# Two mixture-of-experts loops: down products on four 32-column tiles and up weights in runs of eight rows per partition

## The chip, the cores and the metric

The kernel runs on one core of a Trainium2 chip, in float32. The metric is the time of one execution on the device in microseconds. TensorE is called PE in the profile's rows (its weight loads PEld), VectorE DVE, ScalarE ACT, GpSimd POOL and SyncE SP.

## The reference, cut to what matters

The program is two transformer blocks on 1024 tokens of width 1024. Each block ends with a mixture of experts: a router picks two of 32 experts for each token, the pairs are sorted by expert and padded to whole blocks, and each block of tokens goes through one expert.

```python
def moe_ffn(u, rg_w, rg_b, re_w, re_b, w1, w3, w2):
    ...
    xb = u[row_tok].reshape(n_blocks, MOE_BLOCK, u.shape[1])

    def expert_block(args):
        xblk, e = args
        return (jax.nn.silu(xblk @ w1[e]) * (xblk @ w3[e])) @ w2[e]

    yb = lax.map(expert_block, (xb, block_expert)).reshape(n_rows, u.shape[1])
    y = yb[dest] * sw[:, None].astype(u.dtype)
    return jax.ops.segment_sum(y, stok, num_segments=n_tok)
```

In the first block `w1` and `w3` are 32 x 1024 x 512 and `w2` is 32 x 512 x 1024; in the second block (`hier_moe`, the same formula) the hidden width is 256. The input of the experts is the block's normed activation: in the first block `modulate(rms_norm(x, g), shift, scale)`, in the second `rms_norm` with a gain. The first block's result is also multiplied by a gate vector of 1024 elements.

## The kernel before

The kernel cuts the sorted pairs into blocks of 96 tokens (`BT`), and the number of blocks is found at run time: with these inputs 36 in the first loop and 32 in the second. `phase_experts` (L1559) is one function for both, called with a hidden width of 512 (four groups of 128, `HT = 4`) or 256 (`HT = 2`). Its loops run over pairs of blocks, with two slots `s` in every buffer. The engines work by semaphores, each in its own program order:

- SP loads the weights of the next block but one. L1586 moves `w1` and `w3` into `wu[:, s, j]` once TensorE has freed them (`wufree`), then L1588 moves `w2` into `wd` (`wdfree`). All are laid out by `experts_to_tiles` (L158): partition p gets the rows k x 128 + p, k = 0 to 7. Each descriptor is one row, 2 KB or 1 KB of `w1` and `w3`, 4 KB of `w2`.
- POOL fetches the 96 tokens of the next block: it copies the block's column of token numbers (L1605) and issues an indirect transfer of 96 rows of 4 KB from `keep_normed` in DRAM into `xg` (L1607). It starts when TensorE has transposed the tokens that were in the other slot (`xt`).
- TensorE does the up products of block i (L1634: for each of `w1` and `w3`, each group of 128 hidden columns and each k, two products on column tiles of 64, moving operand `uT[:, s, k, :]` of 96 tokens), then `turn` (L1620), eight transposes of the next block's tokens, then waits for `hT` (`gated`), for the weights and for a free result tile (`yout`), and does the down products (L1646): 2 halves of 512 columns x `HT` products with `hT` (128 x 96 tokens) as the stationary operand. They use 96 of the array's 128 columns. In the profile each float32 product is two records (a transpose is one), so the first loop has 256 records at L1634, 8 at L1620 and 16 at L1646 a block.
- ACT does silu of the first up result (L1668), scales the transposed tokens into `uT` with a factor and an addend for each partition and k (L1657), in the second loop copies the results to `yo` (L1677), and issues the transfer of 96 rows to `keep_rows` (L1679).
- DVE multiplies silu by the second up result into `hT` (L1695); in the first loop it also multiplies the result by the gate into `yo` (L1701).

The stationary operand of transpose k is `xg[:, slot, k*P:(k+1)*P]`, 128 neighbouring elements of each token. Input channel k x 128 + p so lands on partition p of group k, where the weights' row k x 128 + p is.

Ahead of each expert loop come the route phase (`phase_mix_route`) and, before it, the merge phase (`phase_merge`), which has a list of copies on POOL's queue: `copy_aside` (L119) issues them one by one; the first `needed` are issued at once, and POOL waits for each later one to land before it issues the next. In the profile `mixed_T` and `b2z_Z` are the memory of `wd` in the first and the second loop; `in_w` as a source in the second loop stands for `w1_2`, `w3_2` and `w2_2`.

## Time and profile before

| | us |
|---|---|
| time, median of 3 runs | 4847.99 |
| lowest and highest | 4840.06, 4849.69 |
| the profiled execution, its own time | 4835.41 |
| its span in the profile | 4833.6 |
| TensorE busy (share of the span) | 4203.8 (87%) |
| DVE busy | 1292.3 (27%) |
| ACT busy | 1027.0 (21%) |
| POOL busy | 467.5 (10%) |
| first expert loop, from and to | 1804.7, 2502.5 |
| second expert loop, from and to | 4429.8, 4786.5 |

The span is 1.8 us shorter than the profiled execution's own time, and that execution is 12.6 us below the median. The page cuts the span into 40 slices of 121 us: the first loop lies in the 16th to the 21st, the second in the last four. Busy shares are means over stages with different limits, so what bounds a loop has to be read from its own rows: from the timeline of one engine, where a bracket behind a row gives the idle time before it and what ended that. A timeline row joins instructions of one kind that follow each other, and its length ends with the last one's end, which may lie behind the start of the next row. A row of the table of stretches has the stretch, its length, the busy time (and number of instructions) of PE, PEld, DVE, ACT and POOL, TensorE's granted clock as a share of 2.4 GHz, the busy share of the DMA engines and their GB/s.

### The profile page before, as it was taken

To read this page: it belongs to the slowest core of one execution; us is meant where nothing else is said; L and a number is where in the kernel's file an instruction comes from. 1 tells how busy PE (TensorE), PEld (TensorE's weight loads), DVE (VectorE), ACT (ScalarE), POOL (GpSimd) and SP (SyncE) were. 2 spreads that over 40 slices of the span, in tenths; PEclk is the share of its full clock that TensorE was granted. 3 is DMA by queue.
4 is the path that set the end of the run, shared out by engine and by line. 5 is a ranking of instruction groups with operands and counts; after the bars stand their busy time and mean duration, and the time that the engine had idled before them with its cause. 6 is when DMAs were issued, how large, how long until landed. Compare 5 with 4: busy or idle time off the path is not lost. (4 is left out here: it accounts for less than half of the span.)

```text
span 4833.6 us, 90330 instructions
## 1 busy us (share of the span) xinstructions
PE 4203.8 (87%) x38805; PEld 2639.6 (55%) x38805; DVE 1292.3 (27%) x2325; ACT 1027.0 (21%) x2418; POOL 467.5 (10%) x672
## 2 busy tenths in 40 slices
PE   7897588987899979999979886998999979997885
PEld 2343244876344447777755443448888834445663
DVE  2425112123000130110123554225665520112002
ACT  2200100013000012211223332014444300012333
POOL 1010000000000000000010000005445400000001
PEclk9999799997899989999989998999999989998998
DMA  5361211000411139999973001100000031115998
GB/s 201 140 184 59 102 39 61 31 14 0 133 46 30 51 104 378 367 369 368 369 280 86 9 5 61 35 17 3 4 4 4 4 116 46 30 60 163 353 351 300
DMA packets 361717, 601.08 MB, mean 124 GB/s; under 512 B 35224, under 2 KB 211895, under 8 KB 358040
## 3 DMA queue, kind: packets, MB, share of 16 engines
q1 hardware_dynamic: 324511, 454.52, 27.9%
q0 software_dynamic: 28592, 115.88, 7.3%
q10 hardware_dynamic: 8394, 27.46, 1.5%
q8 instruction: 174, 2.85, 0.2%
q14 instruction: 46, 0.38, 0.0%
HBM read 522.57 MB, written 75.24 MB: 124 GB/s over the span
## 5 line engine op out<-in xcount | busy, mean ns | idle before, releaser
L1634 PE MATMUL experts_bank<-experts_uT,ex_wu 128*64 128x96 f32 x13312 | 568.5, 247 | 69.7 <-DMA ex_wu<-in_w 41.1
L1634 PEld LDWEIGHTS experts_bank<-experts_uT,ex_wu 128*64 128x64 f32 x13312 | 556.9, 138 | 125.6 <-issue 125.6
L1646 PE MATMUL experts_bank<-mixed_T,experts_hT 128*96 128x512 f32 x576 | 255.9, 597 | 0.0
L1811 PE MATMUL taps_bank<-rwkvh_hT,taps_w 128*128 128x512 f32 x480 | 211.6, 599 | 31.7 <-DMA taps_w<-in_w_in 25.6
L1275 DVE TENSOR_TENSOR merge_pr<-merge_bank,merge_sg 128x512 f32<-128x512 f32 x64 | 44.3, 692 | 709.4 <-ACT merge_sg L1262 435.8
L1695 DVE TENSOR_TENSOR experts_hT<-experts_si,experts_bank 128x384 f32<-128x384 f32 (+1 forms) x68 | 31.3, 460 | 756.6 <-PE experts_bank L1634 756.6
L1248 PE MATMUL merge_bank<-b2m_hT,merge_w 128*128 128x512 f32 x512 | 222.3, 592 | 0.0
L1248 PE MATMUL merge_bank<-mix_h2T,merge_w 128*128 128x512 f32 x512 | 222.3, 592 | 0.0
L1811 PE MATMUL hin_bank<-mix_hT,hin_w 128*128 128x512 f32 x384 | 170.2, 602 | 14.6 <-DMA hin_w<-in_w_in 8.9
L1811 PEld LDWEIGHTS taps_bank<-rwkvh_hT,taps_w 128*128 128x128 f32 x480 | 90.6, 191 | 152.7 <-issue 146.3
L2081 POOL TENSOR_TENSOR rc_lev<-rc_arb,rwkv_level 128x256 f32<-128x256 f32 x192 | 153.8, 834 | 157.3 <-DVE rc_arb L2434 157.2
L1646 PEld LDWEIGHTS experts_bank<-mixed_T,experts_hT 128*96 128x96 f32 x576 | 90.9, 163 | 136.5 <-issue 134.1
L1248 PEld LDWEIGHTS merge_bank<-mix_h2T,merge_w 128*128 128x128 f32 x512 | 97.3, 190 | 122.5 <-issue 122.5
L1248 PEld LDWEIGHTS merge_bank<-b2m_hT,merge_w 128*128 128x128 f32 x512 | 97.3, 190 | 122.5 <-issue 122.5
L1262 ACT ACTIVATE merge_sg<-merge_bank,all_cols 128x512 f32<-128x512 f32 x64 | 44.0, 687 | 546.3 <-PE merge_bank L1248 546.2
L2450 DVE TENSOR_TENSOR rc_xy<-rc_xy,rc_bank 128x256 f32<-128x256 f32 x288 | 120.8, 421 | 122.4 <-PE rc_bank L2095 116.7
L1657 ACT ACTIVATE experts_uT<-experts_bank,all_mod 128x96 f32<-128x96 f32 x296 | 99.5, 442 | 203.9 <-PE experts_bank L1620 203.9
L1248 PE MATMUL merge_bank<-mix_hT,merge_w 128*128 128x512 f32 x256 | 114.9, 602 | 30.2 <-DMA merge_w<-in_hy_w_o 26.0
L327 PE MATMUL vproj_bank<-vproj_w,mix_hT 128*128 128x256 f32 x512 | 114.0, 386 | 23.0 <-DMA vproj_w<-in_w_in 21.6
L1811 PEld LDWEIGHTS hin_bank<-mix_hT,hin_w 128*128 128x128 f32 x384 | 72.9, 192 | 111.4 <-issue 111.4
L2832 PE MATMUL mh_sc<-mla_KTs,mh_QT 128*128 128x512 f32 x256 | 120.7, 594 | 5.1 <-ACT mla_KTs L2877 5.1
L507 PE MATMUL qk_bank<-mix_hT,qk_w 128*128 128x512 f32 x256 | 113.8, 603 | 9.3 <-DMA qk_w<-in_w_in 8.1
(499 smaller groups left out, 6539.5 us busy)
## 6 DMA issues: line engine op xcount, KB each, us to landing
ex_wu<-in_expert_w SPq DMA_DIRECT2D x72, 2048.0 KB, 14.4
mixed_T<-in_expert_w SPq DMA_DIRECT2D x36, 2048.0 KB, 15.4
ex_wu<-in_w SPq DMA_DIRECT2D x64, 1024.0 KB
b2z_Z<-in_w SPq DMA_DIRECT2D x32, 1024.0 KB, 15.9
keep_rows<-experts_yo ACTq DMA_DIRECT2D x68, 384.0 KB, 6.0
keep_rows<-mix_hyT POOLq DMA_DIRECT2D x27, 768.0 KB, 4.7
mix_hT<-in_ada_w POOLq DMA_DIRECT2D x8, 2048.0 KB, 8.6
merge_w<-in_w_in SPq DMA_DIRECT2D x32, 512.0 KB, 5.1
```

Source lines behind the costliest of these rows:

```text
L327: last = pe.matmul(bk[t][:, 0:width], xT[:, k, tok0 + t * P:tok0 + (t + 1) * P], wt[:, s, k, :], start=(k == 0), stop=(k == kt - 1))
L507: last = pe.matmul(bk[2 * s + h][:, :], wt[:, s, k, :], xT[:, k, h * HALF:(h + 1) * HALF], start=(k == 0), stop=(k == KT - 1))
L1248: last = pe.matmul(bk[4 * h + j][:, :], w[:, s, k0 + k, :], x[:, k, hh], start=(k == 0), stop=(k == n - 1))
L1262: act.activation(sg[:, h, j, :], bk[4 * h + j][:, :], ACT.Sigmoid, bias=K.cols[:, bass.ds(i * 2 + (s + gate_col + 8 * j), 1)]).then_inc(si ...
L1275: dve.tensor_tensor(pr[:, h, j, :], bk[4 * h + 2 + j][:, :], sg[:, h, j, :], ALU.mult).then_inc(prod, 1)
L1634: last = pe.matmul(bk[2 + j][c:c + 64, h * BT:(h + 1) * BT], wu[:, s, j, k, h * P + c:h * P + c + 64], uT[:, s, k, :], start=(k == 0), sto ...
L1646: last = pe.matmul(bk[5 + j][0:BT, :], hT[:, k * BT:(k + 1) * BT], wd[:, s, k, j * HALF:(j + 1) * HALF], start=(k == 0), stop=(k == HT - 1))
L1657: last = act.activation(uT[:, slot, k, :], bk[k // 4][:, k % 4 * BT:(k % 4 + 1) * BT], ACT.Identity, scale=scale(k), bias=shift(k) if shif ...
L1811: last = pe.matmul(bk[s * 2 + h][:, :], wt[:, s, k, :], xT[:, k, h * HALF:(h + 1) * HALF], start=(k == 0), stop=(k == KT - 1))
L2081: gp.tensor_tensor(lev[d][:, l, :, :], arb[d][:, :, 0, :], W.level[:, d, l:l + 1, :].to_broadcast([P, J, CH]), ALU.mult).then_inc(pos[d], 1)
L2450: dve.tensor_tensor(xy[d][:, x, :, :], xy[d][:, x, :, :], b2(bk[d][bank]), ALU.add).then_inc(dvs[d], 1)
L2832: last = pe.matmul(sc[g % 2][:, half(x)], QT[:, h % 2, u * P:(u + 1) * P], KTs[:, h // 2 % 2 * 2 + h % 2, half(x)], start=True, stop=True)
```

## The change

The down products go on four tiles of 32 columns instead of one product of 96 columns. The stationary operand is 32 tokens of `hT`. Tiles 0, 1 and 2 take one group of 32 tokens each and columns 0 to 767 of the result (`WIDE`), first 512 and then 256 columns wide. Tile 3 takes columns 768 to 1023 for all three groups of tokens, 256 wide, one group after the other. The results of a block lie in banks 4 + 2s and 5 + 2s instead of always in 5 and 6. `yo` becomes 128 partitions x 768: its partitions 96 to 127 hold the three groups' last quarter. The rows are saved by two transfers, 96 x 768 and 32 x 3 x 256. The gate is laid out in the same way once before DVE's loop (`gt`, four copies).

`w1` and `w3` are laid out by `experts_to_runs`: partition p gets the rows 8p to 8p + 7, which are neighbours in DRAM, so a matrix is 128 descriptors of 16 KB in the first loop and 8 KB in the second. To match, transpose k takes every eighth element of a token, from element k on. Scale and addend for L1657 have to be by the same order: `modrun` is made from `K.mod` by a copy to DRAM (`keep_mod`) and back at the end of the first merge's list of copies, and `ffnrun` by a load at the end of the second's. `w2` stays as it was. The diff, cut to its core:

```diff
             gp.dma_start(dst, src).then_inc(asided, 16)
...
+def experts_to_runs(ap):
+    return ap.rearrange("l e (p k) n -> p (l e) k n", p=P)
...
+OUT = ((0, HALF), (HALF, WIDE))
...
-        yo = m.sb("yo", [BT, 2, D])
+        yo = m.sb("yo", [P, 2, WIDE])
+        gt = m.sb("gt", [P, WIDE]) if gate is not None else None
...
-                    last = pe.transpose(bk[k // 4][:, k % 4 * BT:(k % 4 + 1) * BT], xg[:, slot, k * P:(k + 1) * P], K.ident[0:BT, 0:BT])
+                    last = pe.transpose(bk[k // 4][:, k % 4 * BT:(k % 4 + 1) * BT], xg[:, slot, :].rearrange("q (p k) -> q k p", k=KT)[:, k, :], K.ident[0:BT, 0:BT])
...
+            def quarter(s, j, c, tokens, k, c0, n, at):
+                return pe.matmul(bk[4 + 2 * s + j][32 * c:32 * c + 32, at:at + n], hT[:, k * BT + 32 * tokens:k * BT + 32 * tokens + 32],
+                                 wd[:, s, k, c0:c0 + n], start=(k == 0), stop=(k == HT - 1))
...
                     for j in range(2):
+                        width = HALF if j == 0 else 256
+                        rest = [(t, k) for t in ((0, 1) if j == 0 else (2,)) for k in range(HT)]
                         for k in range(HT):
-                            last = pe.matmul(bk[5 + j][0:BT, :], hT[:, k * BT:(k + 1) * BT], wd[:, s, k, j * HALF:(j + 1) * HALF], start=(k == 0), stop=(k == HT - 1))
+                            for c in range(3):
+                                last = quarter(s, j, c, c, k, j * HALF, width, 0)
+                            for t, q in rest[k * len(rest) // HT:(k + 1) * len(rest) // HT]:
+                                last = quarter(s, j, 3, t, q, WIDE, 256, t % 2 * 256)
                         last.then_inc(ymm, 1)
...
-                        act.activation(yo[:, s, j * HALF:(j + 1) * HALF], bk[5 + j][0:BT, :], ACT.Copy).then_inc(yout, 1)
+                        act.activation(yo[:, s, OUT[j][0]:OUT[j][1]], bk[4 + 2 * s + j][:, 0:OUT[j][1] - OUT[j][0]], ACT.Copy).then_inc(yout, 1)
...
+                    act.dma_start(rows[:, 0:WIDE], yo[0:BT, s, :]).then_inc(saved[s], 16)
+                    act.dma_start(rows[:, WIDE:D].rearrange("(g p) n -> p g n", p=32), yo[BT:P, s, :].rearrange("p (g n) -> p g n", g=3)).then_inc(saved[s], 16)
...
+            if gate is not None:
+                dve.tensor_copy(gt[0:BT, :], gate[0:BT, 0:WIDE]).then_inc(gates, 1)
+                for g in range(3):
+                    dve.tensor_copy(gt[BT:P, g * 256:(g + 1) * 256], gate[BT:P, WIDE:D]).then_inc(gates, 1)
+                dve.wait_ge(gates, 4)
...
-                            dve.tensor_tensor(yo[:, s, j * HALF:(j + 1) * HALF], bk[5 + j][0:BT, :], gate[0:BT, j * HALF:(j + 1) * HALF], ALU.mult).then_inc(yout, 1)
+                            dve.tensor_tensor(yo[:, s, a:z], bk[4 + 2 * s + j][:, 0:z - a], gt[:, a:z], ALU.mult).then_inc(yout, 1)
...
-    ws = tuple(experts_to_tiles(I[w]) for w in (w1, w3, w2))
+    ws = (experts_to_runs(I[w1]), experts_to_runs(I[w3]), experts_to_tiles(I[w2]))
...
+                    + ((S.mod.rearrange("a (k p) -> p a k", p=P), K.mod[:, 2, :, :]), (K.modrun[:, :, :], S.mod.rearrange("a (p k) -> p a k", p=P))), 5)
...
+                        + ((K.ffnrun[:, :], I["norm_ffn_g_2"].rearrange("l (p k) -> p (l k)", p=P)),), 4, crossed=True)
```

What stands in a row on TensorE in the second half of the second loop's body, one block, before (up products, a wait, eight transposes, a wait, four down products):

```order
L1634 MATMUL experts_bank<-experts_uT,ex_wu 64x96 x64
L1637 REGISTER_ALU
L1620 MATMUL experts_bank<-all_ident,ex_xg 128x96 x8
L1641 REGISTER_ALU
L1646 MATMUL experts_bank<-b2z_Z,experts_hT 96x512 x4
L1648 REGISTER_ALU
```

The same place of the changed kernel:

```order
L1649 MATMUL experts_bank<-experts_uT,ex_wu 64x96 x64
L1652 REGISTER_ALU
L1630 MATMUL experts_bank<-all_ident,ex_xg 128x96 x8
L1656 REGISTER_ALU
L1635 MATMUL experts_bank<-b2z_Z,experts_hT 32x512 x3
L1635 MATMUL experts_bank<-b2z_Z,experts_hT 32x256 x2
L1635 MATMUL experts_bank<-b2z_Z,experts_hT 32x512 x3
L1635 MATMUL experts_bank<-b2z_Z,experts_hT 32x256 x10
L1668 REGISTER_ALU
```

The up products and transposes stand as they did. The 4 down products of 96 columns have become 18 of 32: 3 of 512 columns for tiles 0 to 2, then 2 of 256 for tile 3, twice over, and then, joined with these in the last row, 3 of 256 for tiles 0 to 2 and 1 for tile 3, twice over.

ACT in the same half of the body, before (silu, the scaling of the next tokens, the two result copies, the transfer of the rows):

```order
L1668 ACTIVATE experts_si<-experts_bank 128x192
L76 REGISTER_ALU
L1657 ACTIVATE experts_uT<-experts_bank,all_cols 128x96 x8
L1677 ACTIVATE experts_yo<-experts_bank 96x512
L76 REGISTER_ALU
L1677 ACTIVATE experts_yo<-experts_bank 96x512
L1678 REGISTER_ALU
L1679 ISA
L1679 DMA keep_rows<-experts_yo 96x1024
```

And of the changed kernel:

```order
L1688 ACTIVATE experts_si<-experts_bank 128x192
L76 REGISTER_ALU
L1677 ACTIVATE experts_uT<-experts_bank,all_ffnrun 128x96 x8
L1697 ACTIVATE experts_yo<-experts_bank 128x512
L76 REGISTER_ALU
L1697 ACTIVATE experts_yo<-experts_bank 128x256
L1698 REGISTER_ALU
L1700 ISA
L1700 DMA keep_rows<-experts_yo 96x768
L1701 ISA
L1701 DMA keep_rows<-experts_yo 32x3x256
```

The second copy is half as wide as the first, both are 128 partitions high, and behind them stand two transfers instead of one.

## Rows read from the trace of the kernel before

**Rows 1.** The page's line of what the DMA engines moved, in 40 slices.

```profile
GB/s 201 140 184 59 102 39 61 31 14 0 133 46 30 51 104 378 367 369 368 369 280 86 9 5 61 35 17 3 4 4 4 4 116 46 30 60 163 353 351 300
```

**Rows 2.** Table of stretches: both loops, then one block of each.

```profile
1804.70:2502.50 697.80, 671.26 (x10080) 500.30 (x10080) 69.40 (x108) 137.60 (x342) 37.71 (x68) 1.00 1.00 360
4429.70:4786.50 356.80, 313.86 (x4608) 232.25 (x4608) 11.34 (x32) 127.24 (x367) 33.45 (x61) 0.99 1.04 341
2095.03:2114.42 19.39, 18.54 (x280) 13.82 (x281) 2.26 (x4) 3.18 (x9) 1.11 (x2) 1.00 1.02 357
4607.28:4618.57 11.29, 9.75 (x144) 7.20 (x145) 0.35 (x1) 4.64 (x12) 1.10 (x2) 1.00 1.07 353
```

**Rows 3.** TensorE's timeline in the first loop: start, length, line, bracket for idle time.

```profile
2114.42 10.78 PE L1634 MATMUL experts_bank<-experts_uT,ex_wu 128*64 128x96 f32 x256 [0.85 <-PE experts_bank L1646]
2125.14 0.88 PE L1620 MATMUL experts_bank<-all_ident,ex_xg 96*128 96x96 f32 x8
2125.95 7.11 PE L1646 MATMUL experts_bank<-mixed_T,experts_hT 128*96 128x512 f32 x16
```

**Rows 4.** TensorE's timeline in the second loop, early and later.

```profile
4452.69 5.50 PE L1634 MATMUL experts_bank<-experts_uT,ex_wu 128*64 128x96 f32 x128 [0.96 <-PE experts_bank L1646]
4462.86 5.50 PE L1634 MATMUL experts_bank<-experts_uT,ex_wu 128*64 128x96 f32 x128 [0.42 <-PE experts_bank L1646]
...
4612.71 0.88 PE L1620 MATMUL experts_bank<-all_ident,ex_xg 96*128 96x96 f32 x8
4613.43 3.60 PE L1646 MATMUL experts_bank<-b2z_Z,experts_hT 128*96 128x512 f32 x8
4618.57 1.62 PE L1634 MATMUL experts_bank<-experts_uT,ex_wu 128*64 128x96 f32 x34 [1.55 <-DMA ex_wu<-in_w]
```

**Rows 5.** Column tiles of 32 (timeline), and products 256 columns wide (groups by form).

```profile
126.69 1.92 PE L759 MATMUL front_bank<-mix_hyT,front_cc 128*32 128x512 f32 x16 [0.28 <-DMA mix_hyT<-in_ada_w]
...
L327 PE MATMUL vproj_bank<-vproj_w,mix_hT 128*128 128x256 f32 x512 | 114.0, 386 | 23.0 <-DMA vproj_w<-in_w_in 21.6 <-DVE ret_v L3015 0.8 <-PE vproj_bank L327 0.6
```

**Rows 6.** Operands read or written at a step (timeline, groups by form, transposes' loads).

```profile
406.64 1.96 PE L1153 MATMUL hturn_bank<-all_ident,hy_xc 128*128 128x128 f32 x15
...
L1473 DVE TENSOR_TENSOR all_X<-all_X,route_gt 128x512 f32<-128x512 f32 x16 | 11.1, 692 | 0.5
L1503 DVE TENSOR_TENSOR route_A<-route_oh,route_o 128x256 f32<-128x256 f32 x4 | 1.5, 422 | 0.1
L1507 DVE TENSOR_TENSOR route_A<-route_A 128x256 f32<-128x256 f32 x2 | 1.2, 620 | 0.1
...
L1620 PEld LDWEIGHTS experts_bank<-all_ident,ex_xg x560: 137/141/230, 1800.3 to 4782.8; 96*128 96x128 f32 x187
```

**Rows 7.** Stretches 491 to 498, 2103 to 2107; packets 4607.6 to 4610.6, 3903 to 3912.

```profile
491.00:498.00 7.00, 2.89 (x4) 1.35 (x5) 0.00 (x0) 0.00 (x0) 0.00 (x0) 0.50 1.00 428
2103.00:2107.00 4.00, 4.00 (x79) 3.60 (x75) 0.56 (x1) 0.28 (x1) 0.16 (x1) 1.00 1.03 409
...
DMA packets 483, 0.89 MB, mean 297 GB/s; under 512 B 20, under 2 KB 347, under 8 KB 483
q1 hardware_dynamic: 373, 0.50, 60.5%
...
q0 software_dynamic: 468, 3.44, 93.3%
q1 hardware_dynamic: 435, 0.22, 8.5%
```

**Rows 8.** TensorE's and POOL's timelines at a gather, its landing, POOL after merge.

```profile
4601.37 0.88 PE L1620 MATMUL experts_bank<-all_ident,ex_xg 96*128 96x96 f32 x8
...
4603.41 0.94 POOL L1607 DMA_INDIRECT ex_xg<-keep_normed,experts_now  x1 [0.77 <-POOL experts_now L1605]
...
DMA to landing us min/median/max: 7.7/7.8/8.0
...
1627.45 0.31 POOL L1349 MEMSET route_fresh<- 128x256 f32 x1 [376.36 <-POOLq L70]
```

More of the change, by code:

```diff
@@ L126, in _ @@
         for n, (dst, src) in enumerate(pairs):
-            gp.dma_start(dst, src).then_inc(asided, 16)
+            gp.dma_start(dst, src, allow_slow_non_contiguous=True).then_inc(asided, 16)
             if n >= needed - 1:
@@ L1197 @@
 MAXB = 54
+WIDE = 768
 BT = 96
@@ L1572, in phase_experts @@
         saved = m.sems("saved0", "saved1")
-        picked, = m.sems("picked")
+        picked, gates = m.sems("picked", "gates")
         wufree, wdfree, xt, ux, up, sil, gated, ymm, yout = m.sems(
@@ L1675, in _ @@
                         if j == 0:
-                            hold(act, saved[s], i * 16 + 16)
-                        act.activation(yo[:, s, j * HALF:(j + 1) * HALF], bk[5 + j][0:BT, :], ACT.Copy).then_inc(yout, 1)
+                            hold(act, saved[s], i * 32 + 32)
+                        act.activation(yo[:, s, OUT[j][0]:OUT[j][1]], bk[4 + 2 * s + j][:, 0:OUT[j][1] - OUT[j][0]], ACT.Copy).then_inc(yout, 1)
                     act.wait_ge(yout, i * 4 + (2 * s + 4))
-                    act.dma_start(out_dram[bass.ds(i * (2 * BT) + s * BT, BT), :], yo[:, s, :]).then_inc(saved[s], 16)
+                    rows = out_dram[bass.ds(i * (2 * BT) + s * BT, BT), :]
+                    act.dma_start(rows[:, 0:WIDE], yo[0:BT, s, :]).then_inc(saved[s], 16)
+                    act.dma_start(rows[:, WIDE:D].rearrange("(g p) n -> p g n", p=32), yo[BT:P, s, :].rearrange("p (g n) -> p g n", g=3)).then_inc(saved[s], 16)
             for s in range(2):
-                hold(act, saved[s], n * 16 + 16)
+                hold(act, saved[s], n * 32 + 32)
         @b.vector
@@ L1688, in _ @@
             for s in range(2):
-                dve.sem_inc(saved[s], 16)
+                dve.sem_inc(saved[s], 32)
+            if gate is not None:
[3 more added lines that the diff above has]
+                dve.wait_ge(gates, 4)
             with dve.Fori(0, n) as i:
@@ L1699, in _ @@
                             if j == 0:
-                                dve.wait_ge(saved[s], i * 16 + 16)
-                            dve.tensor_tensor(yo[:, s, j * HALF:(j + 1) * HALF], bk[5 + j][0:BT, :], gate[0:BT, j * HALF:(j + 1) * HALF], ALU.mult).then_inc(yout, 1)
+                                dve.wait_ge(saved[s], i * 32 + 32)
+                            a, z = OUT[j]
+                            dve.tensor_tensor(yo[:, s, a:z], bk[4 + 2 * s + j][:, 0:z - a], gt[:, a:z], ALU.mult).then_inc(yout, 1)
 def phase_combine(nc, name, K, X, T, out_dram, gain, out):
@@ L3046, in hyena, with moe @@
         phase_inverse(nc, I, K, prod, xc, hyT)
-def moe(nc, tag, I, K, S, T, w_out, mixedT, spare, mix_gate, hidden, scale, shift, names, gate=None, ahead=None):
+def moe(nc, tag, I, K, S, T, w_out, mixedT, spare, mix_gate, hidden, scale, shift, run_cols, names, gate=None, ahead=None):
     rgw, rgb, rew, reb, w1, w3, w2 = names
-    ws = tuple(experts_to_tiles(I[w]) for w in (w1, w3, w2))
+    ws = (experts_to_runs(I[w1]), experts_to_runs(I[w3]), experts_to_tiles(I[w2]))
     with Mem(nc, f"ex{tag}") as mx:
@@ L3064, in moe @@
         phase_mix_route(nc, f"route{tag}", I, K, K.X, w_out, wide, mixedT, mix_gate, scale, shift, I[rgw], I[rgb], I[rew], I[reb], T, S.normed, *ws)
-        phase_experts(nc, f"experts{tag}", K, hidden, *ws, scale, shift, T, S.normed, S.rows, gate, ahead() if ahead else ())
+        phase_experts(nc, f"experts{tag}", K, hidden, *ws, *run_cols, T, S.normed, S.rows, gate, ahead() if ahead else ())
 def first(nc, I, K, S, T, ahead):
@@ L3092, in first @@
     moe(nc, 1, I, K, S, T, rows_to_tiles(I["w_out"]), mixedT, None, K.gt[:, 0, :], 512, lambda k: K.mod[:, 2, 0, k:k + 1], lambda k: K.mod[:, 2, 1, k:k + 1],
+        (lambda k: K.modrun[:, 0, k:k + 1], lambda k: K.modrun[:, 1, k:k + 1]),
         ("router_group_w", "router_group_b", "router_expert_w", "router_expert_b", "expert_w1", "expert_w3", "expert_w2"), K.gt[:, 1, :], latents)
@@ L3162, in two_blocks @@
         S.hyT = nc.dram_tensor("keep_hyT", [P, 4, SEQ], F32, kind="Internal").ap()
+        S.mod = nc.dram_tensor("keep_mod", [2, D], F32, kind="Internal").ap()
         S.x = nc.dram_tensor("keep_x", [SEQ, D], F32, kind="Internal").ap()
@@ L3165, in two_blocks @@
         S.rows = nc.dram_tensor("keep_rows", [MAXB * BT, D], F32, kind="Internal").ap()
+        K.modrun, K.ffnrun = m.sb("modrun", [P, 2, KT]), m.sb("ffnrun", [P, KT])
         K.mod, K.gt, K.X = m.sb("mod", [P, 3, 2, 8]), m.sb("gt", [P, 2, D]), m.sb("X", [P, KT, D])
```

5 lines of the change are left out of this document (3 added, 2 removed).

## The prediction

> **What bounds the kernel now.** The change touches the two expert loops, so I read those first in the forty slices of the span [rows 1]: the transfers run at 367 to 369 GB/s in the first loop and 351 to 353 in the second. The table of stretches [rows 2] gives 697.8 us for the first loop (36 blocks) and 356.8 us for the second (32 blocks), at the full clock, with the 16 DMA engines busy all the time. That alone would say that transfers are the bound. The timeline of TensorE says otherwise for the first loop.
>
> First loop: one block takes the 19.39 us from 2095.03 to 2114.42 [rows 2]. Inside the next one [rows 3] I see up products in 10.78, eight transposes at 2125.14, and from 2125.95 sixteen records of down products in 7.11. The idle time before a block's up products is 0.85 us at the turn of the loop and about 0.4 in its middle [rows 3, 4], and it ended with TensorE's own last product, so the block from 2114.42 takes 11.53 + 7.11 + 0.4 = 19.0. No row names a transfer. The period is 19.2 us on average and TensorE sets it.
>
> Second loop [rows 4]: an early block takes 10.17 us (4452.69 to 4462.86) and its idle time ends on TensorE itself; with 0.96 of idle time instead of 0.42 the other takes 10.71. Later the period is 11.29 us [rows 2], and 1.55 us of it is a wait for the up weights' transfer. So TensorE's own pace is 10.44 us, the mean, and the transfers set 11.29.
>
> **The change part by part.**
>
> *Down products.* Before, a product is two records. Sixteen take 7.11 us [rows 3]: less about 0.6 for the last one, over 15, 0.43 us each, one after the other. Afterwards four 32-column tiles work side by side. The trace has that form: the products of the first phase on four tiles of 32, 512 columns, show 16 records in 1.92 us [rows 5], so four start together, and a round of four takes (1.92 - 0.6) / 3 = 0.44 us, at the full clock. Each tile now takes 768 columns instead of 1024. With 256 columns a record costs 0.22 us (114.0 us over 512) [rows 5]. First loop: 8 rounds x 0.43 + 8 x 0.22 + 0.2 for the last one's end = 5.4, so 1.7 us off each block. Second loop, half the depth: 4 x 0.43 + 4 x 0.22 + 0.2 = 2.8 against 3.60 [rows 4], 0.8 off. The unknown here is the fourth tile, which gets four short records in place of two long ones. If these overlap as in the row, the sum stands; I take that, since the streams are of equal length. If the fourth tile ran alone, it would add 16 x 0.22 + 8 x 0.22 = 5.3 us a block of the first loop.
>
> *Transposes.* This is what speaks against the change. With eight rows per partition, transpose k must read every eighth element of a token's row: the stationary operand is now read at a step of 32 bytes instead of 4. The trace has one transpose with a step, the 8-byte one of the Hyena branch [rows 6]: 15 records in 1.96 us, less 0.28 for the last (my estimate of its own length), over 14, 0.120 us each, against (0.88 - 0.25) / 7 = 0.09 in the expert loop [rows 3]. For 32 bytes VectorE has a pair of rows [rows 6]: two additions or products of 128x256, 422 ns with a step of 4 bytes and 620 where the result is written at 32 (L1507), so 198 / 256 = 0.77 ns more an element; the unit step costs (692 - 422) / 256 = 1.05, hence 1.8 ns an element at 32 bytes. TensorE at 8 bytes, 120 / 128 = 0.94 ns, is just half of 1.8, which fits a cost by the stretch of memory touched: two elements in each at 8 bytes, one at 32. So I take 1.8 x 128 = 0.23 us for each of the eight stationary loads; the bounds are 0.12 (a step costs the same whatever its size) and about 0.35 (three times the 8-byte row). The load, hidden today (141 ns of record, [rows 6]) behind the moving operand, then sets the pace: the eight transposes' last start moves from 0.63 to about 0.3 + 6 x 0.23 = 1.7 us after the first, and the down products start 1.8 us after the first transpose. Today they start after 0.81 [rows 3] (VectorE's hT ends last) and 0.72 [rows 4]. The price is 1.0 us a block in the first loop and 1.1 in the second, all on TensorE's path.
>
> The Trainium skill, SBUF — State Buffer, section Door 1: The DMA port swizzle, says that SBUF has lines of 16 bytes, that accesses within one line run at full bandwidth and that each crossing to a new line pays. By that rule each of the 128 elements crosses, where at 8 bytes every second one does; the trace's 0.94 and 1.8 ns agree with it, and the sum by the rule is the one above.
>
> *Up weights.* The two loads of a block become 128 runs of 16 KB (first loop) or 8 KB (second) instead of 1024 of 2 KB or 1 KB. Rates: 428 GB/s where 16 KB rows alone move, 409 where 4 KB rows move [rows 7], against 351 to 353 in the second loop. One block of it moves 11.29 x 353 = 3.99 MB. During the gather of the next tokens 0.89 MB pass in 3 us at 297 GB/s [rows 7]; w2 and the saved rows, 1.45 MB, take 3.5 us at 409; so the rest, 1.65 MB, takes 4.8 now and 3.9 at 425. The floor of the transfers falls from 11.3 to 10.4 us. By the same sum the first loop, with 2.5 MB of w2 and results and 3.7 MB of w1 and w3 beside the gather's 0.89, needs 3.0 + 6.1 + 8.7 = 17.8 us against a period of 19.2. There this part gives nothing unless TensorE goes below.
>
> *Gather.* The tokens of the next block are fetched by POOL after a block's transposes. In the second loop: first transpose at 4601.37, the index copy after the last, gather issued at 4603.41, so 2.04 us after the first transpose, and 7.8 us to landing [rows 8]. The next transposes can't start before 2.04 + 7.8 = 9.8 us; today 11.3 covers it. With transposes 1.1 us longer the issue comes 1.1 later: 10.9. That is a new chain, longer than the transfers' floor and than TensorE's own path, 10.44 - 0.8 + 1.1 = 10.7. In the first loop, by the same row, it needs 2.04 + 7.8 + 1.1 = 10.9 of 18.5.
>
> *The rest costs nothing.* The scale and shift by runs are made by three more copies on POOL's queue, at the end of its lists in the two merges; those of the first write and read 2048 elements of 4 bytes. No row has a transfer of such pieces. A 512-byte packet takes 28 ns of an engine (8.5% of 16 x 9 us over 435) [rows 7]; at ten times that, 4096 pieces take 72 us on 16 engines, and after the last of today's copies POOL stands idle for 376.36 us [rows 8]. TensorE waits only for the first five copies, which stay first. Results leave in two transfers instead of one, 0.3 us more of issue on ACT's queue, which waits for TensorE anyway; the second result tile is 256 instead of 512 wide, which shortens VectorE's and ACT's last step. The four copies for the gate stand before VectorE's loop, beside the first 10 us of up products. Without that cover they would cost under 2 us once.
>
> **The sum.** First loop: 36 x (1.7 - 1.0) = 25 us off, period 18.5. Second: from 11.2 to 10.9, 31 x 0.3 = 9 off. The first transposes of each loop stand alone on the path: 2 x 1.0 back. Together 32 us off the profiled execution, 4833.6 to 4801.6 in the span, 4803 in its time of 4835. The median of the runs shown is 4848, so 4816.
>
> **The rivals.**
>
> *The step costs no more than 0.12 us a load (as the 8-byte row).* Then the down products start about 1.0 us after the first transpose, 0.2 to 0.3 later than now. First loop: 36 x 1.45 = 52 off, period 17.8, equal to the transfers' floor. Second: TensorE 9.9, gather 10.1, transfers 10.4, so 31 x 0.8 = 25 off. 77 in all: 4771. For it: it is the only row of TensorE with a step. Against it: VectorE's 32-byte row, and that 8 bytes already cost what half a 1.8 would.
>
> *The gather is starved (slower).* Gather packets of 4 KB share each engine with the weights' queue. In the rows of the second loop's gather 373 packets of weights and results pass beside the other queue's 110, 96 of them the gather's rows [rows 7], nearly four for one. If it stays so with packets of 8 and 16 KB, each of the gather's six packets per engine (96 over 16) waits for some three of 0.31 us (8192 B at 26.8 GB/s, 428 / 16), or of 0.61 in the first loop: 6 x 1.1 = 6.7 us in place of 3, and 6 x 2.0 = 12. Second loop: 10.9 + 3.7 = 14.6, 3.4 x 31 = 105 slower; first loop: 3.1 to the issue (2.04 + 1.1), 7.8 to landing and 9 more, 19.9, and 0.5 until the up products can start: 20.4 against 19.2, 36 x 1.2 = 43 slower; 4848 + 148 = 4996. It decides from a landing of 8.1 us in the second loop and of some 15 in the first. Against it: at the start of the second merge, where POOL's queue moves 8 KB pieces beside 512-byte pieces of the weights, the two queues show 468 and 435 packets [rows 7]: strictly one for one. So a large packet may hold a small one up once, not three times, and four for one means that the gather's descriptors come slowly. One for one gives 6 x (0.31 + 0.17) = 2.9 us in the second loop, as now.
>
> The Trainium skill, DMA: Bandwidth & Descriptors, section Queues, rings and completion order, says that an engine goes round its queues and drains one packet before it switches. The 468 to 435 agree. By the rule a gather packet waits for one weights packet, of whatever size, and the sum above is unchanged; only if a packet held several of the 16 KB runs would it give the starved case.
>
> *No change to be measured.* Loads of 0.27 us or more take back 1.3 of the 1.7 us and put the gather's chain at 11.2: 36 x 0.4 - 2 = 12 us off or less. At 0.35 us the first loop gains nothing and the second loses 0.5 us a block, 15 in all: 4865, with the fourth tile's poor overlap as a worse companion (+5.3 us x 36).
>
> **Numbers.** Forecast (0.23 us a load, four tiles in parallel, gather as now) 0.50; flat step 0.24; loads of 0.27 to 0.35 0.12; starved gather, wholly or in part, or fourth tile 0.14. A measurement here can tell about 0.2%, 10 us. Faster by more than that: 0.50 + 0.24 + 0.02 of the third, less 0.03 for the sum's own error, 0.73; within it 0.11, nearly all from the third; slower 0.16, the last and the end of the third. The range goes from 4757, under the flat case, to 4850, where the third case begins to cost; the fourth case is left out.
>
> **What would show it.** In the changed profile: (1) down records of 32 columns, a burst of 5.4 us (first loop) and 2.8 (second); over 6.5 and the fourth tile doesn't overlap. (2) Eight transposes over some 2.0 us from first start to end, stationary loads of about 320 ns instead of 141 in the record (141 / 0.09 x 0.23 would be 360, 141 + 180 is 320); under 220 means the flat case. (3) Periods of 18.5 us, and 10.9 with idle time before the second loop's transposes that ends on the gather; 10.4 with a wait for the up weights means transfers. (4) Gather landing of about 7.8 us, as now; above 10 the starved case. (5) Nothing else moves: the stretches between the loops keep their lengths within a few us. Wrong would be above all a load price far from 0.23 us, since each 0.05 us of it is worth 0.35 us x 68, 24 us.

## The result, and the profile after

The changed kernel takes 4757.8 us (median of 4 runs, 4750.2 to 4767.1) against 4844.0 (4 runs, 4840.0 to 4849.7): a ratio of 0.9825, interval 0.9812 to 0.9838, some 86 us faster. The prediction was 4816, 32 us faster. The time lies at the low edge of the range, and the gain is 2.7 times the forecast. The nearest case is the first rival (flat step, 4771).

The profiled execution of the changed kernel has a span of 4765.3 us, the slowest of its runs, so the difference of the spans is 68 us and not 86: some 82 us less in the two loops and 14 more in the rest. Of these 14, 11 lie between the last down product of the first loop and the first up product of the second (1942.8 against 1932.1 us). The fifth sign of the prediction had these stretches unmoved within a few us. But e10 below, which has every part of the change, shows 1933.6 there, so the 11 us are put down to the scatter between executions. I read the loops.

The table of stretches (stretch, length, busy time and number of instructions of PE, PEld, DVE, ACT and POOL, clock, DMA share, GB/s): both loops, then one block of each. It answers to [rows 2].

```profile
1808.50:2452.30 643.80, 620.71 (x12096) 530.06 (x12096) 59.80 (x108) 137.35 (x342) 37.55 (x68) 1.00 1.00 389
4394.90:4718.50 323.60, 298.71 (x5504) 248.45 (x5504) 11.34 (x32) 124.69 (x367) 33.31 (x61) 0.99 1.00 376
2097.06:2114.63 17.57, 17.17 (x337) 14.66 (x337) 1.61 (x3) 4.46 (x10) 1.10 (x2) 1.00 1.02 400
4668.00:4678.24 10.24, 9.29 (x172) 7.70 (x173) 0.35 (x1) 3.27 (x11) 1.11 (x2) 1.00 1.02 387
```

356.8 us have become 323.6 in the second loop. For the first, 697.8 and 643.8 can't be compared as they stand: the stretch before runs to 2502.5, and TensorE's last down product ended at 2497.7. From the first up product to the last down product it is 692.9 before and 643.6 after. TensorE's timeline in the first loop, which answers to [rows 3]:

```profile
2114.63 10.78 PE L1649 MATMUL experts_bank<-experts_uT,ex_wu 128*64 128x96 f32 x256 [0.40 <-PE experts_bank L1635]
2125.34 1.13 PE L1630 MATMUL experts_bank<-all_ident,ex_xg 96*128 96x96 f32 x8
2126.39 5.39 PE L1635 MATMUL experts_bank<-mixed_T,experts_hT 128*32 128x512 f32 x72
2132.67 1.54 PE L1649 MATMUL experts_bank<-experts_uT,ex_wu 128*64 128x96 f32 x32 [0.89 <-PE experts_bank L1635]
```

The up products are untouched at 10.78. The down products are a burst of 5.39 us instead of 7.11. They start 1.05 us after the first transpose (1.06 in the median block); the forecast had 1.8. The brackets name TensorE's own last product. Over the loop a block takes 17.80 us on average (17.57 and 18.03 in turn) against 19.21.

The second loop, TensorE and then POOL, which answers to [rows 4, 8]:

```profile
4612.10 1.12 PE L1630 MATMUL experts_bank<-all_ident,ex_xg 96*128 96x96 f32 x8
4613.15 2.80 PE L1635 MATMUL experts_bank<-b2z_Z,experts_hT 128*32 128x512 f32 x36
4616.82 5.50 PE L1649 MATMUL experts_bank<-experts_uT,ex_wu 128*64 128x96 f32 x128 [0.87 <-DMA ex_wu<-in_w]
...
4604.16 0.92 POOL L1617 DMA_INDIRECT ex_xg<-keep_normed,experts_now  x1 [0.77 <-POOL experts_now L1615]
...
DMA to landing us min/median/max: 8.7/9.0/9.1
```

Down products take 2.80 instead of 3.60, and a block 10.11 instead of 11.22. The gather issued at 4604.16 lands some 9.0 us later, at 4613.2. The transposes at 4612.10 start before that, with no idle time. So they don't need this gather. That is the first crack in the prediction.

### The profile page after: what moved, and what is told of

Same layout as the page of the kernel before. It is cut to its first block and busy times, and to the rows that moved or that the text cites. A ratio compares the mean times of both kernels' runs of the same rounds, so it can differ in the third digit from the quotient of the medians.

```text
span 4765.3 us, 96365 instructions
## 1 busy us (share of the span) xinstructions
PE 4151.1 (87%) x41717; PEld 2692.9 (57%) x41717; DVE 1283.6 (27%) x2329; ACT 1023.2 (21%) x2418; POOL 469.3 (10%) x675
## 5 line engine op out<-in xcount | busy, mean ns | idle before, releaser
L1635 PE MATMUL experts_bank<-mixed_T,experts_hT 128*32 128x256 f32 (+1 forms) x2592 | 193.9, 451 | 0.0
L1635 PEld LDWEIGHTS experts_bank<-mixed_T,experts_hT 128*32 128x32 f32 x2592 | 110.4, 110 | 69.6
L1677 ACT ACTIVATE experts_uT<-experts_bank,all_modrun 128x96 f32<-128x96 f32 x296 | 99.3, 439 | 212.6 <-PE experts_bank L1630 212.6
```

The source lines that it names most:

```text
L1635: return pe.matmul(bk[4 + 2 * s + j][32 * c:32 * c + 32, at:at + n], hT[:, k * BT + 32 * tokens:k * BT + 32 * tokens + 32], wd[:, s, k, c0 ...
L1677: last = act.activation(uT[:, slot, k, :], bk[k // 4][:, k % 4 * BT:(k % 4 + 1) * BT], ACT.Identity, scale=scale(k), bias=shift(k) if shif ...
```

## The experiments

All periods below are means over a loop's blocks without the first three and the last, from the starts of the up products in each profiled execution. The column before the last is the time from a block's first transpose to its first down product, in both loops unless two values stand.

| kernel | ratio to before | loop 1, us a block | loop 2, us a block | first transpose to down | down burst, loop 1, 2 |
|---|---|---|---|---|---|
| before | 1 | 19.21 | 11.22 | 0.76 (0.72 and 0.81 in turn), 0.72 | 7.11, 3.60 |
| changed | 0.9825 | 17.80 | 10.11 | 1.06 | 5.39, 2.80 |
| e1 tiles only | 0.9931 | 18.45 | 11.21 | 0.81 | 5.39, 2.80 |
| e2 runs only | 0.9970 | 19.33 | 10.62 | 0.97 | 7.03, 3.60 |
| e3 plain transposes | 0.9851 (34 blocks) | 17.56 | 10.27 | 0.81 | 5.39, 2.80 |
| e4 runs of 2 | 0.9851 | 17.87 | 10.48 | 1.13 | 5.39, 2.80 |
| e5 runs of 4 | 0.9834 | 17.88 | 10.11 | 1.13 | 5.39, 2.80 |
| e6 late gather | one run | 17.81 | 10.02 | 1.06 | 5.39, 2.80 |
| e9 no drain | 0.9804 | 17.48 | 10.18 | 1.06 | 5.39, 2.80 |
| e10 no drain, runs of 4 | 0.9811 | 17.62 | 10.21 | 1.13 | 5.39, 2.80 |
| e11 changed again | 0.9830 | 17.83 | 10.15 | 1.06 | 5.39, 2.80 |
| e12 fourth last | one run | 19.60 | 10.16 | 1.06 | 7.20, 2.82 |

**The two parts apart.** e1 keeps the old layout of the weights:

```diff
-    ws = (experts_to_runs(I[w1]), experts_to_runs(I[w3]), experts_to_tiles(I[w2]))
+    ws = tuple(experts_to_tiles(I[w]) for w in (w1, w3, w2))
...
-                    last = pe.transpose(..., xg[:, slot, :].rearrange("q (p k) -> q k p", k=KT)[:, k, :], K.ident[0:BT, 0:BT])
+                    last = pe.transpose(..., xg[:, slot, k * P:(k + 1) * P], K.ident[0:BT, 0:BT])
```

> The four column tiles alone: weights, transposes and scale as before the change. Theory: the step is gone, so down products start 0.8 us after the first transpose and take 5.4 us (first loop) and 2.8 (second). First loop: TensorE alone would need 19.2 - 1.7 = 17.5 us a block, but transfers in 2 KB pieces need about 18, so the period is 17.9 to 18.3: 36 x 1.1 = 40 us off. Second loop: transfers set 11.2 as before, nothing off. About 4804 against 4844, ratio 0.992. Rival (transfers bound the first loop as well, at 19.2): no change, ratio 1.000. Rival (the tiles made all of the measured gain): ratio 0.983.

Measured: 4810.6 us, ratio 0.9931 (0.9914 to 0.9948), close to the 0.992 expected. The second loop did not move. The first fell to 18.45, a little above the 17.9 to 18.3 expected. TensorE's timeline at one block and at the start of a later one, the waits in the stretch 1850 to 2430 (in all, times, longest), then the stretches of the first block's up products, of the first loop and of the second:

```profile
2099.70 12.44 PE L1649 MATMUL experts_bank<-experts_uT,ex_wu 128*64 128x96 f32 x256 [2.38 <-DMA ex_wu<-in_expert_w]
2112.06 0.88 PE L1630 MATMUL experts_bank<-all_ident,ex_xg 96*128 96x96 f32 x8
2112.87 5.39 PE L1635 MATMUL experts_bank<-mixed_T,experts_hT 128*32 128x512 f32 x72
...
2248.26 10.78 PE L1649 MATMUL experts_bank<-experts_uT,ex_wu 128*64 128x96 f32 x256 [2.96 <-DMA ex_wu<-in_expert_w]
...
PE experts_bank L1649 <- DMA ex_wu<-in_expert_w: 28.3, 15, 3.3
...
2099.80:2112.10 12.30, 12.30 (x257) 12.18 (x257) 0.00 (x0) 1.77 (x2) 0.00 (x0) 0.86 1.04 389
1850.00:2430.00 580.00, 542.93 (x10555) 462.73 (x10554) 52.32 (x94) 121.00 (x303) 35.53 (x64) 0.98 1.04 383
4450.00:4690.00 240.00, 204.81 (x3704) 170.50 (x3704) 7.79 (x22) 82.82 (x250) 23.97 (x44) 0.96 1.07 353
```

Now the first loop waits for the up weights: 15 times, 28.3 us in 580. The up products that follow the wait of 2.38 us run at a granted clock of 0.86 and take 12.44 us instead of 10.78 (over the loops 0.98 and 0.96). This wait so costs 1.66 us more than its own length. Not every wait does: the one of 2.96 us before 2248.26 is followed by up products at 10.78. In this stretch six blocks have slow up products (12.1 to 13.7 us), each behind a wait of 2.3 us or more; they cost 10.9 us together, about 0.35 us a block.

e2 is the other half: the runs with the strided transposes, and the old `L1646` products with a `yo` of 96 rows.

> The runs of eight rows alone, with the strided transposes, down products as before the change. Theory: down products start 1.06 us after the first transpose instead of 0.81 and 0.72. First loop 19.2 + 0.3 = 19.5, 36 x 0.3 = 10 us slower; second loop now at TensorE's own pace, 10.44 + 0.34 = 10.8 against 11.2, 13 us faster. Sum near zero: ratio 0.997 to 1.001. Rival (the runs made the second loop's gain by themselves, whatever TensorE does): second loop 10.2, 32 us faster, ratio 0.995. Rival of the prediction on record (0.23 us a load): first transpose to down products 1.8 us, ratio above 1.005.

Measured: 4829.2 us, ratio 0.9970 (0.9960 to 0.9980), at the edge of what was expected. The first loop is 0.12 us a block slower, the second 0.60 faster, at TensorE's own pace (no wait of its TensorE there ends on a transfer). One block of the first loop:

```profile
2104.90 1.13 PE L1629 MATMUL experts_bank<-all_ident,ex_xg 96*128 96x96 f32 x8
2105.86 7.03 PE L1655 MATMUL experts_bank<-mixed_T,experts_hT 128*96 128x512 f32 x16
```

The step costs 0.12 us a block here and not the 0.3 I had expected: the time to the down products is 0.97 instead of a mean of 0.76, and the burst is 0.08 shorter.

One part alone saves 32 us, the other 14; both together save 81 to 86. The sum is off because each loop has two limits close together. In the second, tiles alone leave the transfers' 11.21, runs alone leave TensorE's 10.62, and only both give 10.11. In the first, tiles alone run into the transfers, and into the lost clock behind some of the waits, at 18.45.

**The price of the step.** e3 is the changed kernel with plain transposes (the diff's second hunk above). It computes something else: weights meet the wrong channels.

> The changed kernel, but the transposes read 128 neighbouring elements as before, so the weights' rows meet the wrong channels: what it computes is not the reference's, the work is the same. Theory: stationary loads of 141 instead of 206 ns in the record, down products start 0.8 us after the first transpose; first loop 17.8 - 0.3 = 17.5, 10 us off; second loop early blocks 9.6, late ones at the transfers' 10.3: 3 us off. 13 us below the changed kernel, ratio to before 0.980. Rival (17.8 in the first loop is already the transfers' floor): nothing off, ratio 0.9825 as the changed kernel.

Measured: 4771.1 us. Its other activations give the second router 34 blocks instead of 32, so 2 x 10.27 us have to come off, which leaves 4750.6, 7 us under the changed kernel; 13 were expected. The first loop can be compared directly: 17.56 against 17.80, where 17.5 was expected. The step costs 0.24 us a block there, and the transfers allow 17.56. The second loop gained nothing: at 10.27 us its TensorE waits for the weights in every block, and it is 0.16 us above the changed kernel's 10.11, for a reason that is not settled. e4 and e5 change its size, with the layout of the weights to match (for e4):

```diff
-    return ap.rearrange("l e (p k) n -> p (l e) k n", p=P)
+    return ap.rearrange("l e (b p r) n -> p (l e) b (r n)", p=P, r=2)
...
-xg[:, slot, :].rearrange("q (p k) -> q k p", k=KT)[:, k, :]
+xg[:, slot, :].rearrange("q (b p r) -> q b r p", b=4, r=2)[:, k // 2, k % 2, :]
```

> The changed kernel with runs of two rows per partition: transposes at a step of 8 bytes instead of 32, up weights in pieces of 4 KB (first loop) and 2 KB (second). Theory (a step costs the same whatever its size): stationary loads of 206 ns as at 32 bytes, down products 1.06 us after the first transpose. First loop 17.8 as the changed kernel; second loop, transfers in 2 KB pieces, between 10.3 and 11.2, about 10.7. Ratio 0.985 to 0.987. Rival (cost by the memory touched, half at 8 bytes): loads well under 206 ns and a first loop of 17.5 to 17.6.

> The changed kernel with runs of four rows per partition: transposes at a step of 16 bytes, up weights in pieces of 8 KB (first loop) and 4 KB (second). Theory (a step costs much the same whatever its size: 113 ns a transpose at 32 bytes, 120 at 8): 0.11 to 0.12 us a transpose here, first loop 17.8. Second loop, with pieces of 4 KB: 10.2 to 10.3, against 10.1 at 8 KB and 10.5 at 2 KB. Ratio 0.982 to 0.984. Rival (the piece's size counts up to 8 KB as much as from 2 to 4 KB): second loop 10.3 to 10.4, ratio over 0.984.

Measured: ratios 0.9851 (0.9835 to 0.9868) and 0.9834 (0.9814 to 0.9854). The stationary loads of the transposes (count, then least, median and largest record in ns): changed kernel (32 bytes), e4 (8 bytes), e5 (16 bytes), e1 (4 bytes).

```profile
L1630 PEld LDWEIGHTS experts_bank<-all_ident,ex_xg x560: 185/206/226, 1804.1 to 4715.4; 96*128 96x128 f32 x187
```

```profile
L1630 PEld LDWEIGHTS experts_bank<-all_ident,ex_xg x560: 194/217/231, 1800.3 to 4718.0; 96*128 96x128 f32 x187
```

```profile
L1630 PEld LDWEIGHTS experts_bank<-all_ident,ex_xg x560: 195/217/230, 1803.5 to 4715.2; 96*128 96x128 f32 x187
```

```profile
L1630 PEld LDWEIGHTS experts_bank<-all_ident,ex_xg x560: 137/141/231, 1801.2 to 4756.2; 96*128 96x128 f32 x187
```

A step costs 65 to 76 ns more in the record whatever its size, and 32 bytes are a little cheaper than 8 or 16, not dearer; why is open. From start to start the single records show 83 ns for a transpose without a step, 120 at 8 and 16 bytes and 111 at 32 (the first of the eight takes longer: 0.14 us without a step and 0.19 with one). The rival of e4 falls. For pieces of 1, 2, 4 and 8 KB the second loop takes 11.21 (e1), 10.48 (e4), 10.11 (e5) and 10.11 us: the gain is over at 4 KB, where e5's expectation still had 0.1 to 0.2 us more than at 8 KB. TensorE's own path is about 9.9 us here (5.43 + 1.06 + 2.80 and 0.64 idle), only 0.2 less, so this pair alone could hide a gain; but e9 and e10 below, where that path is some 0.3 us shorter, hardly differ either (10.18 with 8 KB, 10.21 with 4 KB).

**The gather.** e6 holds the gather back without a byte more of traffic:

```diff
                     hold(gp, picked, i * 2 + (s + 1))
+                    for q in range(6):
+                        gp.memset(pad[:, :], 0.0).then_inc(padded, 1)
+                        hold(gp, padded, i * 12 + (6 * s + q + 1))
```

> The changed kernel, but POOL writes 128x512 zeros into a scratch tile six times, one after the other, between the index copy and the gather, so the gather is issued some 4 us later, with no more transfers. Theory (a slot's gather has two blocks' time, since xg has two slots): 2.3 + 4 + 9.0 = 15.3 us from transposes to landing against 20.2 in the second loop and 35.6 in the first: no period changes. Rival (the step of the prediction on record: one block's time): second loop 15.3 us a block instead of 10.1, 32 x 5.2 = 166 us slower than the changed kernel; first loop unchanged.

Measured: 4767.8 us in one run; the second loop takes 10.02 us a block, the first 17.81. POOL's and then TensorE's timeline, and the landings:

```profile
4607.08 3.74 POOL L1620 MEMSET experts_pad<- 128x512 f32 x6
4611.59 0.93 POOL L1622 DMA_INDIRECT ex_xg<-keep_normed,experts_now  x1 [0.77 <-POOL experts_pad L1620]
...
4605.44 1.13 PE L1635 MATMUL experts_bank<-all_ident,ex_xg 96*128 96x96 f32 x8
...
4615.13 1.13 PE L1635 MATMUL experts_bank<-all_ident,ex_xg 96*128 96x96 f32 x8
...
DMA to landing us min/median/max: 8.0/8.2/8.4
```

The gather now leaves 6.2 us after its transposes and lands at 4619.8, long after the next transposes have started at 4615.13. No wait of TensorE in either loop ends on a gather. `xg` has two slots, and the gather that follows block i's transposes fetches tokens for the transposes after the next. It has two periods, some 20 us in the second loop, and needs 11.3 in the changed kernel (2.3 to the issue, 9.0 to landing). The one-period chain of the prediction doesn't exist.

**How near the transfers are.** e7 and e8 leave out seven of eight k of the w3 products (their output is not the reference's) in the changed kernel and in e1, so TensorE has time to spare:

```diff
-                            for k in range(KT):
+                            for k in range(KT if j == 0 else 1):
```

> The changed kernel without seven of eight k of the w3 products (the output is not the reference's); all transfers stay. TensorE needs 4.7 us less a block in the first loop and 2.4 in the second, so the transfers set both periods. Theory: 17.3 to 17.6 us in the first loop, just below the 17.8 of the changed kernel, and 10.2 in the second. Rival (transfers have much to spare in the first loop): under 16.5.

> The tiles-only kernel, without seven of eight k of the w3 products (the output is not the reference's): the transfers' floor with the old layout of up weights. Theory: 18.2 to 18.4 us in the first loop, as in the tiles-only kernel (18.45, which also lost clock), and 11.2 in the second. With the floor at 8 rows a run this tells what the layout is worth by itself: about 0.9 us a block in both loops. Rival (tiles-only's 18.45 was mostly lost clock): 17.5 or less in the first loop.

Measured, in one run each: 17.94 and 10.23 us a block with runs, 18.64 and 11.14 with the old layout. Stretches 1850 to 2430 and 4450 to 4690 of e7, and its waits in the first of them:

```profile
1850.00:2430.00 580.00, 441.40 (x7177) 360.06 (x7173) 53.41 (x96) 120.52 (x306) 34.49 (x63) 0.89 1.02 395
4450.00:4690.00 240.00, 184.91 (x2758) 146.38 (x2756) 8.50 (x24) 92.22 (x276) 26.54 (x48) 0.92 1.02 384
...
PE experts_bank L1649 <- DMA ex_wu<-in_expert_w: 119.7, 29, 7.4
```

The layout by itself is worth 0.7 us of transfer time a block in the first loop and 0.9 in the second; 0.9 in both was expected. Both rivals fall. But 17.94 and 18.64 are each above what was expected (17.3 to 17.6 and 18.2 to 18.4), and 17.94 is above the 17.80 of the changed kernel, the 17.56 of e3 and the 17.48 of e9 below, which all move the same bytes. With a shorter TensorE the transfers were slower, 395 against 403 GB/s. So such a kernel shows a limit of the transfers only to some 3%. Why, is not settled.

**What else stood in the period.** e9 takes away TensorE's wait for its own last product. SP waits for the down products itself:

```diff
-                sp.wait_ge(wdfree, free)
+                sp.wait_ge(ymm, down)
...
-                    pe.wait_ge(ymm, i * 4 + (2 * s + 3))
-                    pe.sem_inc(wdfree, 1)
```

> The changed kernel, but TensorE no longer waits for its own last down product before it goes on: SP waits for the down products' semaphore itself before it loads w2. Theory: the idle 0.40 us before each block's up products shrinks to about 0.05 and 0.5 at the turn of the loop, so TensorE's pace is 17.45 and 9.6; but the transfers stand at 17.6 to 17.9 and 10.1, so the first loop gains 0.1 to 0.2 us a block and the second nothing: 0 to 8 us below the changed kernel, ratio to before 0.981 to 0.9825. Rival (the first loop was all TensorE's): 0.35 us a block, 12 us off and more, ratio 0.979 or less.

> The edit of the run before on top of runs of four rows (8 KB and 4 KB pieces). TensorE's pace is 0.08 us a block longer (120 ns a transpose at 16 bytes), which the first loop then shows only if TensorE still bounds it. Theory (transfers bound both loops, at the same 17.6 to 17.9 and 10.1): the same time as the run before within 5 us. Rival (pieces of 16 KB give the first loop more rate): 3 to 8 us slower than the run before.

> The changed kernel itself once more, beside the two above on the same chip: ratio to before 0.9825 as before. It is what they are compared with.

Measured: e9 4747.6 us (4744.3 to 4750.8), ratio 0.9804 (0.9789 to 0.9819); e10 4751.2, ratio 0.9811 (0.9795 to 0.9828); the changed kernel again on that chip 4760.3 (4754.8 to 4764.1), ratio 0.9830 (0.9815 to 0.9846). e9 is the fastest kernel of this study, 12.7 us under the changed one. TensorE's timeline in its first loop, and the stretch 1850 to 2430:

```profile
2106.26 10.78 PE L1648 MATMUL experts_bank<-experts_uT,ex_wu 128*64 128x96 f32 x256 [0.34 <-issue]
2116.97 1.12 PE L1629 MATMUL experts_bank<-all_ident,ex_xg 96*128 96x96 f32 x8
2118.03 5.39 PE L1634 MATMUL experts_bank<-mixed_T,experts_hT 128*32 128x512 f32 x72
2123.81 10.78 PE L1648 MATMUL experts_bank<-experts_uT,ex_wu 128*64 128x96 f32 x256 [0.39 <-DMA ex_wu<-in_expert_w]
...
1850.00:2430.00 580.00, 569.20 (x11180) 486.63 (x11178) 55.09 (x99) 127.04 (x315) 35.33 (x64) 1.00 1.02 403
```

The first loop gains 0.35 us a block (17.83 to 17.48), all of it, where I had given the transfers' limit as 17.6; the rival was right there in its 0.35 us a block and its 12 us, though the ratio of 0.9804 is not quite its 0.979. The bracket behind 2123.81 names the weights: in this stretch of e9 TensorE waits for them 13 times, 7.5 us in all, against 6 times and 5.2 us in e11 and never in the first trace of the changed kernel. So the first loop's limit of the transfers begins to show at 17.5 to 17.8. The second loop, at its transfers' limit, gains nothing.

e10 is 3.6 us slower than e9, and their times overlap. Both of its forecasts allow that (within 5 us; 3 to 8 us slower), so the total doesn't decide between them. The first loop is 0.14 us a block slower, and TensorE's transposes explain 0.07 of that.

**The fourth tile.** e12 writes tile 3's products behind the others of each half:

```diff
                             for c in range(3):
                                 last = quarter(s, j, c, c, k, j * HALF, width, 0)
-                            for t, q in rest[k * len(rest) // HT:(k + 1) * len(rest) // HT]:
-                                last = quarter(s, j, 3, t, q, WIDE, 256, t % 2 * 256)
+                        for t, q in rest:
+                            last = quarter(s, j, 3, t, q, WIDE, 256, t % 2 * 256)
```

> The changed kernel with tile 3's down products written after all those of tiles 0 to 2 in each half, instead of between them. Theory (instructions start in program order, a product of a free tile is not fetched from far behind): tile 3's work is no longer covered, 16 and 8 short records in the first loop, of which only the end can lie beside the next half: the burst of down products grows from 5.4 to between 8 and 10.5 us in the first loop (period 21 to 23) and from 2.8 to 4 to 5.5 in the second (11 to 12.5). Rival (each tile's work runs ahead whatever the order in the program): 5.4 and 2.8 as now.

Measured: 4827.2 us in one run. TensorE in the first and the second loop:

```profile
2114.62 7.20 PE L1635 MATMUL experts_bank<-mixed_T,experts_hT 128*32 128x512 f32 x72
...
4612.51 2.82 PE L1635 MATMUL experts_bank<-b2z_Z,experts_hT 128*32 128x512 f32 x36
```

Neither theory holds alone. In the second loop, where 12 records of the others stand ahead of tile 3's first in the first half, nothing is lost. In the first loop, where 24 do, the burst is 7.20 us, as long as before the change. By the single records of the trace, tile 3's first product there starts 1.76 us after the burst's start, when 15 of the 24 records ahead of it have started and nine have not; these 1.76 us are what the burst is longer. In the second loop it starts 0.04 us after the burst's start, when 3 of the 12 have started: again nine have not. So work of a free tile does run ahead of its place, by nine records, three rounds of three, in both cases.

## Why the prediction was right or wrong

- **What bounds the loops**: right. TensorE set the first loop and the transfers the second, which e1 shows (second loop unmoved) and e2 (first loop unmoved but for the step).
- **Down products**: right to 0.01 us. 5.4 and 2.8 were forecast from [rows 5], 5.39 and 2.80 measured, and the fourth tile overlapped in full. Without its interleaved order it would not have in the first loop (e12).
- **The step of the transposes**: this is the term that failed. 0.23 us a load was taken, 0.12 measured: (1.13 - 0.27) / 7, as the 8-byte row was read (e4, at 8 bytes, repeats that row's 0.12 from start to start). The price put on it was 1.0 us a block in the first loop and 1.1 in the second; it is 0.24 (e3) in the first. In the second, down products start 0.34 us later than before (1.06 against 0.72), and the transfers cover it. The wrong move was to take the middle value from VectorE's rows [rows 6], another engine that writes, when the only row of TensorE with a step, the 8-byte one, said 0.12. That an element should cost half as much at 8 bytes as at 32 was a pattern read into two numbers of two engines. By the rule of the Trainium skill, SBUF — State Buffer, section Door 1: The DMA port swizzle, that each crossing to a new line of 16 bytes pays, as I applied it, a step of 16 or 32 bytes would cost twice one of 8. The same passage asks for two accesses in a line for full bandwidth, which a step of 8 bytes has with elements of 4, so that this step could also have been read as free. The loads of 217, 217 and 206 ns at 8, 16 and 32 bytes, against 141, agree with neither reading, and the measurement decides.
- **The gather's chain**: wrong. "The next transposes can't start before 2.04 + 7.8 = 9.8 us" leaves out that `xg` has two slots; the waits in the code say so, and e6 shows it. With the chain, the second loop's forecast was 10.9; without it 10.7, by TensorE's own path with the step at its wrong price; with the step right as well 10.4, by the transfers' floor; and 10.1 came. That floor was too high by 0.3, less for its rate (3.99 MB in 10.4 us are 384 GB/s, 387 were measured) than for its bytes: 3.99 MB were read from one block that took 11.29 us, and a block of the changed kernel moves 10.11 x 387 = 3.91 MB.
- **The sum with the measured terms**: first loop 36 x 1.41 = 51, second 31 x 1.11 = 34, together 85 against 86 measured. That they agree to 1 us is luck, since executions of one kernel lie 17 to 21 us apart (4750.2 to 4767.1 after, 4829.0 to 4850.5 before, on one chip each). The forecast had 25 and 9: it missed 26 us in the first loop, by the step alone, and 25 in the second, by the step, the chain and the floor.
- **The rivals.** The flat step was right in mechanism (down products "about 1.0 us after the first transpose", period 17.8 in the first loop) and got 0.24 of the chance where it should have had most. Its 4771 is 13 above the result: 9 by the second loop's floor, and 4 because it starts from 4848 where the runs beside the result have 4844. The starved gather: with packets of 8 and 16 KB the gather landed later, 11.2 us instead of 8.4 in the first loop and 9.0 instead of 7.8 in the second. It is not starved: by the single packets, the 96 rows pass in 3.9 us in the second loop, not 6.7, beside some 98 other packets of 4 KB or more, one for one. The size is not the whole cause either, since e9 has the same packets and a median of 7.6 us in the first loop. The 9.0 us are above the 8.1 from which the case was to decide and cost nothing, since the chain doesn't exist. With two periods a landing could decide from some 18 us in the second loop (20.2 less 2.3, an estimate that no run tests).
- **The layout of the weights** in the first loop: "there this part gives nothing unless TensorE goes below". TensorE did go below, to a pace of 17.5 to 17.8. The old layout's limit is 18.45 to 18.64 there (e1, e8), so the runs are worth 0.65 us a block of the first loop (e1 against the changed kernel), and a tiles-only version would have kept 32 of the 86 us.

## What to carry to other kernels

Where TensorE and the transfers stand within a few per cent of each other, cost both limits for each part of a change and for the whole: here the parts gave 32 and 14 us alone and 81 to 86 together. Take a price from the same engine, even when the row is of another size, before one from another engine that seems to fit. And count the slots of a buffer before you chain a transfer to the period: with two slots, it has two.

## What the runs showed of the hardware

- A stationary load read at a step costs 206 to 217 ns in the record instead of 141, at 8, 16 and 32 bytes alike; eight transposes then take 1.13 to 1.20 us instead of 0.88.
- After a wait of 2.38 us for weights in an otherwise full loop the next up products ran at a mean granted clock of 0.86 and took 15% longer, 12.44 us instead of 10.78; after one of 2.96 us in the same loop they took 10.78 (e1).
- The fourth 32-column tile started a product while nine records of the other three tiles that stand ahead of it in the program had not started, in both loops; with 24 ahead it stood idle for 1.76 us first (e12).
- The four 32-column tiles work side by side: in the down burst of the first loop a round with 512 columns takes 0.43 us and one with 256 columns 0.22, and all 72 records 5.39 us, against 7.11 for the 16 records of 96 columns before.
- In the second loop larger pieces of the up weights, 1, 2 and 4 KB, helped (11.21, 10.48, 10.11 us a block), and 8 KB helped no further (10.11).
